# A hybrid decoder step on one core: the projections in the order dt, xbc, z, v, u, ga, gb, with the branch work between their chunks

## The reference, cut to what matters

```python
h = rmsnorm(x, W['mix_pre_g'][l]) * (1 + sc1) + sh1
z, xbc, dt_raw, u, v, ga, gb = split_cols(h @ W['w_in'][l], IN_SIZES)
ya, hs, cs = ssd_branch(z, xbc, dt_raw, conv0[l], ssm0[l], ...)
yb, vr = chunk_mlp_branch(jax.nn.gelu(u), jax.nn.gelu(v), ...)
merged = jax.nn.sigmoid(ga) * (ya @ W['w_ssd_out'][l]) + jax.nn.sigmoid(gb) * (yb @ W['w_cmlp_out'][l])
x = x + g1 * rmsnorm(merged @ W['w_o'][l], W['mix_post_g'][l])
```

## Time and profile before

| | us |
|---|---|
| median of 3 runs (1924.02 to 1928.8) | 1926.07 |
| the profiled execution | 1930.64 |
| its span, first to last instruction | 1928.3 |
| TensorE busy | 1761.1 |
| VectorE busy | 1336.6 |
| ScalarE busy | 1028.2 |
| GpSimd busy | 68.1 |

### The profile page before, as it was taken

The page is one execution under the profiler, slowest core; times in us unless marked ns, Lnnn a source line. Parts: engine busy times, 40 slices in busy tenths (PEclk is TensorE's granted clock), DMA queues, the critical chain, the costliest instruction groups (busy, mean ns, idle before and its releaser), DMA issues.

```text
span 1928.3 us, 33789 instructions
## 1 busy us (share of the span) xinstructions
PE 1761.1 (91%) x13192; PEld 1634.2 (85%) x13192; DVE 1336.6 (69%) x1658; ACT 1028.2 (53%) x1045; POOL 68.1 (4%) x108
## 2 busy tenths in 40 slices
PE   6999979769999879997786999999999999999995
PEld 4888978658989869987685899989898989899993
DVE  3355767754445456786756688878887888788884
ACT  2344734333333335473342676767676776777771
POOL 4000110000000000020000000000000000000000
PEclk8999988889999979998886899999999999999997
DMA  9897652347886526573240999999999999999980
GB/s 282 259 279 239 204 165 66 120 129 221 282 284 207 163 67 196 165 223 128 66 137 28 311 351 348 357 294 351 347 348 313 337 347 348 334 319 353 344 308 23
DMA packets 379497, 465.06 MB, mean 241 GB/s; under 512 B 10403, under 2 KB 351603, under 8 KB 379378
## 3 DMA queue, kind: packets, MB, share of 16 engines
q1 hardware_dynamic: 372370, 441.65, 70.1%
q0 software_dynamic: 6720, 20.86, 3.5%
q10 hardware_dynamic: 304, 1.08, 0.2%
HBM read 452.84 MB, written 10.92 MB: 240 GB/s over the span
## 4 chain that ended last, share of the span: by engine, by line
PE 79%; DVE 11%; ACT 4%; DMA 4%; issue 2%; POOL 0%; SPq 0%; ACTq 0%; DVEq 0%; POOLq 0%
PE psum L403 9%; PE psum L1143 9%; PE psum L1148 9%; PE psum L1145 9%; PE psum L414 9%; PE psum L408 8%; PE psum L1167 4%; PE psum L1171 4%; PE psum L1168 4%; PE psum L746 2%; PE psum L443 2%; DMA ce<-in_state_ssm_dram 1%; PE psum L1102 1%; DVE ce L1755 1%; DMA out_ssm_s_dram<-ce 1%
## 5 line engine op out<-in xcount | busy, mean ns | idle before, releaser
L369 DVE TENSOR_TENSOR wlo<-raw,whi 128x2048 fp32r<-128x2048 f32 x219 | 501.6, 2291 | 107.9 <-ACT whi L364 107.0
L364 ACT ACTIVATE whi<-raw 128x2048 fp32r<-128x2048 f32 x219 | 418.4, 1912 | 31.6 <-PE psum L1171 30.0
L347 DVE TENSOR_TENSOR wlo<-raw,whi 128x2048 fp32r<-128x2048 f32 x113 | 258.9, 2291 | 247.2 <-ACT whi L342 246.7
L403 PE MATMUL psum<-xhi,whi 128*128 128x264 f32 x1584 | 232.6, 301 | 39.5 <-ACT xhi L1231 37.1
L342 ACT ACTIVATE whi<-raw 128x2048 fp32r<-128x2048 f32 x113 | 216.9, 1919 | 89.8 <-PE psum L414 64.5
L403 PEld LDWEIGHTS psum<-xhi,whi 128*128 128x128 f32 x1584 | 211.8, 198 | 62.0 <-issue 48.1
L408 PE MATMUL psum<-xlo,whi 128*128 128x264 f32 x1584 | 214.3, 289 | 0.0
L414 PE MATMUL psum<-xhi,wlo 128*128 128x264 f32 x1584 | 211.1, 286 | 0.0
L408 PEld LDWEIGHTS psum<-xlo,whi 128*128 128x128 f32 x1584 | 205.5, 195 | 0.0
L1143 PE MATMUL psum<-whi,hghi 128*128 128x256 f32 x1408 | 202.4, 286 | 3.2 <-issue 2.3
L414 PEld LDWEIGHTS psum<-xhi,wlo 128*128 128x128 f32 x1584 | 197.9, 188 | 0.1
(11 more groups left out here) (354 smaller groups left out, 1911.8 us busy)
## 6 DMA issues: line engine op xcount, KB each, us to landing
raw<-in_exp_wd_dram SPq DMA_DIRECT2D x76, 1024.0 KB, 5.1
raw<-in_exp_wg_dram SPq DMA_DIRECT2D x72, 1024.0 KB, 6.7
raw<-in_exp_wu_dram SPq DMA_DIRECT2D x72, 1024.0 KB, 6.9
raw<-in_w_in_dram SPq DMA_DIRECT2D x52, 1024.0 KB, 5.3
raw<-in_w_mod_dram SPq DMA_DIRECT2D x17, 1024.0 KB, 5.5
hf<-in_exp_wu_dram SPq DMA_DIRECT2D x16, 1024.0 KB, 6.5
hf<-in_exp_wg_dram SPq DMA_DIRECT2D x16, 1024.0 KB, 6.7
hf<-in_exp_wd_dram SPq DMA_DIRECT2D x12, 1024.0 KB, 4.9
```

The lines of the kernel that those rows point to most:

```text
L347: dve.tensor_tensor(wlo[slot], raw[slot], whi[slot].bitcast(F32), ALU.subtract) \
L364: act.activation(whi[j % R3], raw6[slot], ACT.Copy).then_inc(sem["hi_ready"], 1)
L369: dve.tensor_tensor(wlo[j % R3], raw6[slot], whi[j % R3].bitcast(F32), ALU.subtract) \
L403: pe.matmul(out, whi[slot][:, k, j * P:(j + 1) * P], hi(k), start=first and k == 0, stop=False)
```

## The change

The projections run as dt, xbc, z, v, u, ga, gb, and what hung behind gb is put between the chunks:

- dt first; softplus under xbc; the convolution from the second xbc chunk to the last z chunk, in nine pieces. The spread of per-head values and of the spatial diagonal comes behind the fifth xbc chunk.
- Behind the z chunks: the convolution's tail, the transposes of the spatial weights (`wT` is now a tile of its own), of the samples' B and C, and the first sample's row.
- Samples: rows 1 to 4 behind the v chunks, 5 behind u1, 6 and 7 behind ga0 and ga1. ScalarE now also multiplies the state by the decay (`scale`, 8 operations in place on the state) beside `outer`; VectorE's `sample` is one addition of 1024 columns, two products by C of 512, and one reduction of 1024. The ring has three buffers (the third is `hT`, first used for the spatial weights). The state b+2 is fetched behind the store of b.
- v's mean and squares under u, its scale under ga0; the affine step of the layer norm moves from VectorE to ScalarE (8 `Identity` activations); its transposes behind ga1 and ga2, the spatial products behind ga3 and gb0.
- The first 128 tokens' transposes behind gb1, their cum spread behind gb2, their exponentials on ScalarE ahead of gb3's epilogue.
- Behind gb: cmlp_out chunk 0, y and state of the first tokens, chunk 1 (with the second tokens' transposes between its parts), cum spread, chunks 2 and 3, y and state of the second tokens.
- GpSimd multiplies ce by C (two products of 1024 columns) in VectorE's place; the exponentials are issued and signalled in halves.
- `modraw[0]` moves to the memory of `sgb`; softplus scratch to that of `sga`; the spatial weights are loaded ahead of the tail's stores; phases that were hardware loops in layer 1 (v, u and others) are unrolled.

The diff at its core:

```diff
-        for name in ("xbc", "dt", "v", "u", "z", "ga", "gb"):
+        for name in ("dt", "xbc", "z", "v", "u", "ga", "gb"):
...
+        ORDER = [("s", 0), ("o", 0)] + [(what, b) for b in range(1, 5) for what in "os"] \
+            + [("o", 5), ("s", 5), ("s", 6), ("s", 7), ("o", 6), ("o", 7)]
...  # GpSimd
+                pool.wait_ge(sem["w_turned"], l + 1)
+                fetch_state(2)
+                pool.wait_ge(sem["tail_out"], 32 * (l + 1))
+                fetch_state(0)
+                fetch_state(1)
+                for b in range(B):
+                    pool.wait_ge(sem["s_new"], l * B + b + 1)
+                    pool.dma_start(new[b], sring[b % SR3]).then_inc(s_out[b % SR3], 16)
+                    if 1 <= b < B - 2:
+                        pool.wait_ge(s_out[(b - 1) % SR3], 16 * (l * PER[(b - 1) % SR3] + (b - 1) // SR3 + 1))
+                        pool.wait_ge(sem["samp_used"], l * B + b)
+                        fetch_state(b + 2)
...
+                for g in (1, 0):
+                    pool.wait_ge(sem["ce_exp"], 2 * (l + 1) - g)
+                    ins = pool.tensor_tensor(ce[:, g * R:(g + 1) * R, :], ce[:, g * R:(g + 1) * R, :],
+                                             bc(xcv[:, KT + G + g, Q:2 * Q], 1, [P, R, Q]), ALU.mult)
...  # TensorE
+                for name, after in (("xbc", after_xbc), ("z", after_z), ("v", lambda c: sample_rows(c + 1)), ("u", after_u),
+                                    ("ga", after_ga), ("gb", after_gb)):
+                    pe_phase(pe, (name, l), IN_CHUNKS[name], xs(xhi), xs(xlo), T, after=after)
...
+                cmlp_chunk(0)
+                y_and_state(0)
+                cmlp_chunk(1, next_tokens)
+                spread_cum(1)
+                cmlp_chunk(2)
+                cmlp_chunk(3)
+                y_and_state(1)
...  # ScalarE
+                def scale(b):
+                    act.wait_ge(s_in[b % SR3], 16 * (l * PER[b % SR3] + b // SR3 + 1))
+                    for k in range(KT):
+                        ins = act.activation(sring[b % SR3][:, k, :], sring[b % SR3][:, k, :], ACT.Copy,
+                                             scale=spx[:, k, b:b + 1])
+                    ins.then_inc(sem["outer_ready"], 1)
...
+                def after_v(c):
                     outer(c + 1)
+                    scale(c + 1)
+                def after_u(c):
+                    if c == 1:
+                        act.wait_ge(sem["v_centered"], l + 1)
+                        act.activation(hf[:, :, :], vb[:, :, :], ACT.Square).then_inc(sem["v_sq"], 1)
+                        outer(5)
+                        scale(5)
+                    if c == 2:
+                        scale(6)
+                    if c == 3:
+                        scale(7)
...  # VectorE
+                def sample(b):
+                    s = b % 2
+                    Sb = sring[b % SR3]
+                    Cb = ms[:, s, G * P:2 * G * P].rearrange("p (g n) -> p g n", g=G)
+                    dve.wait_ge(sem["outer_ready"], OUT[b] + 2 * l * B)
+                    dve.tensor_tensor(Sb, Sb, sprod[s], ALU.add).then_inc(sem["s_new"], 1)
+                    dve.wait_ge(sem["s_new"], l * B + b + 1)
+                    for g in range(G):
+                        ks = slice(g * KT // G, (g + 1) * KT // G)
+                        ins = dve.tensor_tensor(sprod[s][:, ks, :], Sb[:, ks, :], bc(Cb[:, g, :], 1, [P, KT // G, NS]), ALU.mult)
+                    then(ins)
+                    dve.tensor_reduce(ysm[:, :, b], sprod[s], AX.X, ALU.add).then_inc(sem["samp_used"], 1)
```

More of the change, by code:

```diff
@@ L471, in mod_keep, with act_phase @@
                 .then_inc(sem["mod_added"], 1)
-        def act_phase(act, key, count, epilogue=None, peel=0, end=False, after=None):
+        def act_phase(act, key, count, epilogue=None, peel=0, end=False, after=None, ahead=None):
             n0, q0 = N0[key], Q0[key]
@@ L857, in _ @@
[L857 to L864, removed]
                 def sample_rows(b):
-                    if b == 1:
-                        pe.wait_ge(sem["v_inv"], l + 1)
+                    if b == 0:
+                        pe.wait_ge(sem["w_ready"], l + 1)
+                        pe.wait_ge(sem["bc_ready"], l + 1)
@@ L889, in after_gb @@
[L889 to L900, removed]
@@ L920, in _, with spatial @@
-                pe.wait_ge(sem["w_ready"], l + 1)
-                pe.matmul(ms[:, 0, 0:2 * KT], ones[0:KT, :], diag[:, :, :].rearrange("g a b -> g (a b)"), start=True,
-                          stop=True).then_inc(sem["sp_bcast"], 1)
-                pe.wait_ge(sem["sp_bcast_ready"], l + 1)
-                for c in range(NQ):
+                def spatial(c, b0):
                     for k in range(KT):
-                        out = ms[:, 2 * c + k // 4, (k % 4) * Q:(k % 4 + 1) * Q]
+                        out = ms[:, b0 + k // 4, (k % 4) * Q:(k % 4 + 1) * Q]
@@ new lines, in decays, with after_gb, ahead_gb @@
+                    act.activation(mix[:, 0:R, :], mix[:, 0:R, :], ACT.Exp).then_inc(sem["mix_exp"], 1)
+                def after_gb(c):
+                    if c == 2:
+                        keep_b(0)
+                def ahead_gb(c):
+                    if c == 3:
+                        decays(0)
+                        act.wait_ge(sem["sp_taken"], l + 1)
+                        act.wait_ge(sem["w_used"], N0["cmlp_out", l])
+                        hi_of_x(5 * l + 2, ub)
+                gates("z", zs, ACT.Silu, after_z)
@@ new lines, in _ @@
+                gates("v", vb, ACT.Gelu_apprx_tanh, after_v)
+                gates("u", ub, ACT.Gelu_apprx_tanh, after_u)
+                act.wait_ge(sem["v_inv"], l + 1)
+                act.activation(rs[:, 0, :], rs[:, 0, :], ACT.Sqrt).then_inc(sem["v_rs"], 1)
+                gates("ga", sga, ACT.Sigmoid, after_ga)
+                gates("gb", sgb, ACT.Sigmoid, after_gb, ahead_gb)
+                n = N0["cmlp_out", l]
+                split_hi(act, n + 1, 0)
+                split_hi(act, n + 2, 0)
@@ L1667, in _ @@
                     .then_inc(acc_free[q % 2], 1)
-                cum, dt, dta, e_, r_, s2, p_, mx = (dth[:, k, :] for k in range(8))
+                cum, dt = dth[:, 0, :], dth[:, 1, :]
+                dta, e_, r_, s2, p_, mx = (soft[:, k, :] for k in range(6))
                 dve.wait_ge(acc_free[q % 2], q // 2 + 1)
@@ L1774, in after_gb, with after_ga @@
+                def after_ga(c):
                     if c == 0:
                         dve.wait_ge(sem["v_rs"], l + 1)
[L1776 to L1781 removed]
@@ new lines, in after_ga @@
+                    if c == 1 or c == 2:
+                        sample(5 + c)
+                    if c == 3:
+                        for part in ((3,) if l else (1, 2)):
+                            finish_mod(l, part)
+                        dve.wait_ge(sem["v_normed"], l + 1)
+                        dve.wait_ge(sem["sp_bcast_ready"], l + 1)
+                        g0 = tmp[:, 0:KT, :]
+                        then(dve.tensor_tensor(g0, vb[:, :, S:T], bc(spc[:, 0, :], 2, [P, KT, B]), ALU.mult))
+                        then(dve.tensor_tensor(g0, g0, bc(spc[:, 1, :], 2, [P, KT, B]), ALU.add))
+                        dve.tensor_tensor(ub[:, :, S:T], ub[:, :, S:T], g0, ALU.mult)
```

559 lines of the change are left out of this document (294 added, 265 removed).

## The result

The changed kernel takes 1941.72 us (median; 1938.33 to 1944.33), the kernel before 1927.96 in the same session: ratio 1.0072, 95% interval 1.0057 to 1.0087. The forecast was 1899, in a range of 1878 to 1924. It was wrong in sign.

A forecast was written before the change was run, and what follows sets the result against it. It took TensorE, busy 91% of the span, as the bound, with handoff waits behind the projections. Gains of 12.1 (layer 1) and 15.4 us (layer 0), 27.5 together, gave 1903.1, or 1899 on the median's scale; range 1878 to 1924.

The forecast's parts named there:

- What is late instead: Stalls in the mixers from late weight splits and sample work: 17.2 us in layer 1, 10.0 in layer 0.
- TensorE alone: TensorE's time per layer if nothing were late: 246.4 us in layer 1, 276.3 in layer 0.
- Layer 1's stalls: TensorE's waits: behind z3 2.1, u3's weights 1.9, before ga1 5.4, before ga2 2.9, small ones 4.9; 17.2 us in all.
- the slow clock: At the layer's start, the first products run at half speed, costing 1.9 us more.
- Transfers in layer 0: States passing beside w_mod in layer 0's v chunks: 4 us added, bounds 0 and 9.
- Costs taken at nothing: Second y products' mask and ce hidden behind cmlp_out chunks 2 and 3; GpSimd products 2 us, reduction 1.22.
- the slower one: Rival: the ring of states sets the pace, 40 us lost against the 27 gained: 1939 us, chance 0.10.
- half lost to transfers: Rival: slow v and u chunks and late states in layer 0 take half the gain: 1912 us, chance 0.18.
- My sentence of failure: The prediction fails if the projections grow by more than the 38 us that leave the second stretch.

The follow-up runs named there:

- both copies moved: The changed kernel with mod_rows ahead of the sample work on ScalarE and mod_keep ahead of the next split on VectorE (v and u chunks): 1913.5 us.
- small states: The changed kernel with loads and stores of the samples' states cut to one tile of eight, all compute kept: 1942.3 us.

## Why the prediction was wrong

**The failed step** is in "What is late instead": for layer 0 it took v1 as late by "nothing", because a chunk there is 7.46 us and not 5.80 and tile 11 in time, u3's weights as "covered in layer 0", with no reason given, and its stalls as 10.0 in all. The extra 1.66 us were counted as cover for ScalarE. They are w_mod products, and they come with two deadlines of their own, `mod_rows` and `mod_keep`, in the queues that the sample work was moved into. I walked the queues for the weight splits alone. In numbers (a forecast for a part of a layer is, here and below, the prediction's terms added up to that point), z3's end to ga1 in layer 0 was forecast at 82.6 us and took 111.7; with both copies moved it took 85.0, and the layer 295.3 against a forecast of 290.3.

- **TensorE alone and z3.** z3 ends 67.7 us after the first product in layer 1 (forecast 67.6) and 83.8 in layer 0 (85.2). Right: the convolution and softplus did fit beside xbc and z.
- **Layer 1's stalls.** TensorE's and ScalarE's waits of layer 1, 709.40 to 979.42, changed kernel:

```profile
PE psum L404 <- ACT whi L343: 14.0, 5, 6.2
PE psum L404 <- ACT xhi L1289: 5.6, 4, 2.7
...
```

```profile
ACT ce L1350 <- DMA ce<-in_state_ssm_dram: 6.3, 2, 4.7
```

  The five waits are those forecast in their places: 2.35 before v1 (2.1), 1.44 before u0 (0.7), 1.67 before u3 (1.9), 6.19 before ga1 (5.4), 2.34 before ga2 (2.9). The largest is the fetch of state 7, as worked out: ScalarE waited 4.7 for it. ga1 starts 78.4 after z3 (77.8). In layer 1 the method held.
- **Layer 1's clock.** The gain there was 5.7, not 12.1; the layer took 270.0 against 263.6. From ga1 to ga2 it took 12.6 (11.4), from ga2 to the end of gb3 54.1 (51.1), from there on 57.2 (55.8). This is the second step that failed: the sum went by products at full speed behind each stall. TensorE's timeline shows otherwise, behind the 6.19 and behind the spread of cum:

```profile
855.51 3.86 PE L404 MATMUL psum<-xhi,whi 128*128 128x264 f32 x16 [6.19 <-ACT whi L343]
859.17 2.89 PE L409 MATMUL psum<-xlo,whi 128*128 128x264 f32 x16
...
868.07 2.17 PE L404 MATMUL psum<-xhi,whi 128*128 128x264 f32 x16 [2.34 <-ACT whi L343]
```

```profile
909.27 4.60 PE L912 MATMUL psum<-dth,ident 16*128 16x128 f32 x32 [1.02 <-issue]
913.80 3.89 PE L404 MATMUL psum<-xhi,whi 128*128 128x264 f32 x16
917.49 2.76 PE L409 MATMUL psum<-xlo,whi 128*128 128x264 f32 x16
```

  Sixteen products take 3.9, then 2.8 to 2.9, against 2.2 and 2.1: some 2.4 us each time. The granted clock is 0.50 from 856 to 860 and from 914 to 918 us. Behind the 2.34 before ga2 nothing was lost (2.17). The prediction had priced the slow clock for the layer's start only.
- **The affine step** was sized at 2.6 (eight at 0.33). It took 4.1: `859.99 4.10` for the eight of line 1402 on ScalarE, 0.51 each. `scale` was sized at 2.15 and takes 2.3 to 2.5; the reduction takes 1.22, as taken.
- **Transfers in layer 0.** I added 4 us. ScalarE did not wait for a state there in the changed kernel, which is slow enough to hide every transfer (151 GB/s from 140 to 160). With the chain opened, w_mod loads are late by 1.3 and 0.2, and the fetch of state 7 takes 7.3 us (206.41 to 213.74) for the 6.4 of the forecast: some 2.4 us, within the bounds of 0 and 9. The stall before ga1 is 5.4 there for the 3.4 forecast; that the rest of it is due to transfers is not shown.
- **Costs taken at nothing.** Right: TensorE waits for neither mix nor ce before the second y products. VectorE and GpSimd, layer 0 of the changed kernel:

```profile
340.37 3.40 DVE L348 TENSOR_TENSOR wlo<-raw,whi 128x2048 fp32r<-128x2048 f32 x1
343.69 4.55 DVE L1970 TENSOR_TENSOR mix<-mix,btc 128x1024 f32<-128x1024 f32 x2
```

```profile
339.25 2.37 POOL L723 TENSOR_TENSOR ce<-ce,xc 128x1024 f32<-128x1024 f32 x1 [63.53 <-ACT ce L1429]
343.31 2.71 POOL L723 TENSOR_TENSOR ce<-ce,xc 128x1024 f32<-128x1024 f32 x1 [1.70 <-ACT ce L1439]
```

  GpSimd's products take 2.37 and 2.71, within the bounds. The split beside them takes 3.40 in place of 2.29, the two masks 4.55, where those of the first tokens, with GpSimd idle, take 2.35: 1.1 and 2.2 us longer. Layer 1 shows the same (3.41 and 4.54). When the split starts, GpSimd's product has 1.25 us left (to 341.62); when the masks start, 2.33 (to 346.02). So VectorE did stand still for about the rest of GpSimd's product. The 3.3 us lie under cmlp_out chunks 2 and 3, and TensorE waits for nothing from there to the norm, so they cost the sum nothing. The Trainium skill, "SBUF — State Buffer", section "Who interferes with whom", says that a VectorE instruction with two SBUF inputs and a GpSimd instruction that reads SBUF lock each other out for a whole instruction; these rows agree with it.
- **The rivals.** The time, 1941.7, is near that of the slower one (1939), and its reason is not: the ring of states does not set the pace of layer 0 (small states: no gain). Nor was it half lost to transfers. The rival that came true, a deadline of w_mod behind the sample work, I had not named. My sentence of failure, projections that grow by more than leaves the second stretch, is what happened in layer 0.

## What to carry to other kernels

When work is moved into a loop, walk each in-order queue for every handoff of that loop, the shortest too: a copy of 0.2 to 0.4 us behind a long operation can close a chain over three engines. If one wait is removed and an equal one appears elsewhere, look for a second copy of the same chain before giving up the reason: each of the two moves alone left the kernel slower than before, both together made it faster. And price a recurring stall with the slower clock behind it, which here cost almost as much as the idle time itself.

## What the runs showed of the hardware

The granted clock can fall without a pause of TensorE. The rows behind the spread of cum, above, had 1.0 us of idle time ahead of them; behind the second spread of layer 1 (941.56) there is none, and sixteen products take 3.2 and 2.7. In the kernel with both copies first, TensorE's timeline of layer 0 has no idle time at all here:

```profile
92.06 1.07 PE L444 MATMUL psum<-mix,cT 128*32 128x256 f32 x16
93.06 1.95 PE L947 MATMUL psum<-spin,spread 16*128 16x17 f32 x16
94.87 0.37 PE L950 MATMUL psum<-diag,ones 8*128 8x16 f32 x2
95.17 3.33 PE L404 MATMUL psum<-xhi,whi 128*128 128x264 f32 x16
98.30 2.57 PE L409 MATMUL psum<-xlo,whi 128*128 128x264 f32 x16
```

The granted clock is 0.50 from 96 to 98 us, which is 1.2 of 2.4 GHz:

```profile
96.00:98.00 2.00, 2.00 (x11) 2.00 (x10) 0.48 (x1) 1.49 (x1) 0.00 (x0) 0.50 0.91 305
```

Ahead of all these places stand matmuls over 8 or 16 partitions. In the changed kernel the same instructions run at 1.00 (89 to 99 us), and of the nine kernels that have them the profiled executions of five show the slower products behind them (3.3 to 3.7 us for the first sixteen) and four do not (2.2). So this differs from run to run; of the 295.3 us of layer 0 above, some 1.6 us are of this kind. No run was made to find out why.
